# Forty modulation blocks at the start, and gate grids as two rounded products

## The reference, cut to what matters

```
mod = silu(c) @ ada_w[l] + ada_b[l]             # 6 x 1024 values
sh1, sc1, g1, sh2, sc2, g2 = split(mod, 6)
h = rmsnorm(x) * (1 + sc1) + sh1
x = x + g1 * hybrid_mixer(h)                    # four kinds of heads: indexed with a
                                                # T5 bias, rotary latent, forgetting, S5
h = rmsnorm(x) * (1 + sc2) + sh2
x = x + g2 * peer_ffn(h)                        # 128 x 128 experts, 8 heads x top 16
```

## Time and profile before

| what | value |
|---|---|
| median of 3 runs | 2213.9 us (2213.44 to 2215.03) |
| profiled execution, its own time | 2213.12 us |
| span of its instructions | 2211.3 us |
| busy: TensorE, VectorE, ScalarE, GpSimd | 96%, 70%, 56%, 20% |
| transfers | 378.81 MB, mean 171 GB/s |

### The profile page before, as it was taken

How to read it: one execution, slowest core, us unless ns; L and a number is a source line. 1 busy time by engine, 2 the same in 40 slices (tenths; PEclk the granted TensorE clock), 3 DMA queues, 4 the chain that set the end, 5 groups by cost and what they waited for, 6 DMA issues and landing times.

```text
span 2211.3 us, 39875 instructions
## 1 busy us (share of the span) xinstructions
PE 2118.7 (96%) x13716; PEld 1934.7 (87%) x13716; DVE 1543.2 (70%) x3008; ACT 1234.4 (56%) x2348; POOL 440.1 (20%) x184
## 2 busy tenths in 40 slices
PE   5799899999999999999999999999999999999997
PEld 4688789999999998888878978999999998888886
DVE  7688548991778877777768944899177886555554
ACT  8623544554888864444443344455488886545543
POOL 0000046988100000000000005698810000000000
PEclk9899999999999999999999999999999999999999
DMA  7723244555444467777763324455544445666563
GB/s 263 285 81 129 84 139 136 173 169 188 151 137 135 147 201 268 262 261 264 261 213 109 124 68 140 136 171 170 182 153 133 144 142 170 191 194 193 191 193 101
DMA packets 103476, 378.81 MB, mean 171 GB/s; under 512 B 11488, under 2 KB 11872, under 8 KB 102880
## 3 DMA queue, kind: packets, MB, share of 16 engines
q1 hardware_dynamic: 102672, 373.74, 51.2%
q10 hardware_dynamic: 720, 4.00, 0.5%
HBM read 375.46 MB, written 2.23 MB: 171 GB/s over the span
## 4 chain that ended last, share of the span: by engine, by line
PE 74%; issue 9%; POOL 8%; DVE 4%; ACT 2%; DMA 2%; POOLq 0%; ACTq 0%; SPq 0%; DVEq 0%
PE bank L1760 32%; PE bank L1669 8%; PE bank L1670 8%; PE bank L1671 8%; POOL split_lo L478 7%; PE bank L1733 5%; PE bank L1406 4%; DMA ring<-stream 2%; PE bank L1418 1%; PE bank L1657 1%; PE bank L1368 1%; ACT diag L536 1%; PE bank L1431 1%; PE bank L1442 1%; PE bank L1379 1%
## 5 line engine op out<-in xcount | busy, mean ns | idle before, releaser
L1669 PE MATMUL bank<-h_hi,split_hi 128*128 128x256 f32 x2304 | 666.5, 289 | 23.3 <-POOL split_lo L478 11.1
L1671 PE MATMUL bank<-h_hi,split_lo 128*128 128x256 f32 x2304 | 652.1, 283 | 0.0
L1670 PE MATMUL bank<-h_lo,split_hi 128*128 128x256 f32 x2304 | 652.0, 283 | 0.0
L1669 PEld LDWEIGHTS bank<-h_hi,split_hi 128*128 128x128 f32 x2304 | 441.8, 192 | 30.0 <-POOL split_lo L478 16.8
L478 POOL TENSOR_TENSOR split_lo<-ring,split_hi 128x1024 fp32r<-128x1024 f32 x168 | 433.3, 2603 | 172.9 <-ACT split_hi L686 172.7
L1266 DVE TENSOR_TENSOR split_lo<-ring,split_hi 128x1024 fp32r<-128x1024 f32 x248 | 303.8, 1225 | 222.0 <-ACT w_hi L784 222.0
L783 ACT ACTIVATE split_hi<-ring 128x1024 fp32r<-128x1024 f32 x248 | 263.2, 1061 | 343.0 <-PE bank L1760 339.3
L1670 PEld LDWEIGHTS bank<-h_lo,split_hi 128*128 128x128 f32 x2304 | 442.3, 192 | 0.0
L1671 PEld LDWEIGHTS bank<-h_hi,split_lo 128*128 128x128 f32 x2304 | 441.6, 192 | 0.0
L686 ACT ACTIVATE split_hi<-ring 128x1024 fp32r<-128x1024 f32 x296 | 298.7, 1051 | 196.8 <-PE bank L1671 196.7
L1760 PE MATMUL bank<-split_hi,w_hi 128*128 128x512 f32 x1024 | 315.9, 390 | 0.0
(11 more groups left out here) (271 smaller groups left out, 2526.7 us busy)
## 6 DMA issues: line engine op xcount, KB each, us to landing
ring<-stream SPq DMA_DIRECT2D x658, 512.0 KB, 3.5
ada_ring<-stream SPq DMA_DIRECT2D x48, 512.0 KB, 4.3
spill<-tables ACTq DMA_DIRECT2D x1, 1152.0 KB, 4.3
tables<-spill ACTq DMA_DIRECT2D x1, 1152.0 KB, 6.8
xT<-x_in SPq DMA_DIRECT2D x1, 1024.0 KB, 9.5
s5raw<-s5w ACTq DMA_DIRECT2D x2, 512.0 KB, 5.6
y_out<-hT SPq DMA_DIRECT2D x1, 1024.0 KB, 3.9
KM<-mixc SPq DMA_DIRECT2D x1, 576.0 KB, 7.7
```

The source lines that it names most:

```text
L1669: mm(dst, hi, x_hi, start=start, stop=False, skip_group_check=not group)
L1670: mm(dst, hi, x_lo, start=False, stop=False, skip_group_check=not group)
L1671: return mm(dst, lo, x_hi, start=False, stop=stop, skip_group_check=not group)
```

## The change

**Start.** Layer 0's modulation is folded for five chunks only, 40 blocks; the sixth (g2, which is used at the very end of the layer) moves into the value loop of layer 0 ahead of layer 1's six. `pos` and `K` are issued right after `V`, `xT`, `S` and `KM` after the ring. All 31 `ge` have places of their own in `grid`: four are written first, then one after each fold. Chunk sums stand after buckets 10, 15, 20 and 25 and after the last; the squares of x are made by ScalarE after six sets of diagonals and summed after bucket 9, the root stands after twelve sets, and VectorE's norm right behind the folds. The rope arguments go behind the S5 phases, their sine behind `cosT` and ahead of the copy of `aq0`, their products with `mul` ahead of `krA`, and the bias tables (`t5`) behind hT.

**Gate grids.** The gate is split into a rounded high and a low part (VectorE, from PSUM). `hots` are fp32r; `hotA` is scaled by the high part; GpSimd writes four rows a quad scaled by the low part (`hot_lo`, one buffer of four) and waits for the grid before. TensorE makes two rounded products a token that add up in PSUM.

**Value loop.** Turns of 16 rows, seven of them with eight folds each, two accumulators in turn, and each chunk's sums in the middle of the next turn.

```diff
+FIRST_ADA = 5 * KT
+SKIP = ADA - FIRST_ADA
+TURN = 16
@@ sync
             sp.dma_start(V[:, :], vec).then_inc(vec_in, 16)
+            sp.dma_start(posi, pos).then_inc(pos_in, 16)
+            sp.dma_start(K[:, :], consts).then_inc(const_in, 16)
             for s in range(RING):
                 sp.dma_start(ring[:, s, :], stream[s]).then_inc(slot_filled[s], 16)
...
+            sp.dma_start(xT[:, :, :], x_in).then_inc(x_loaded, 16)
+            sp.dma_start(S[:, :, :], small).then_inc(small_in, 16)
             sp.dma_start(KM[:, :], mixc).then_inc(mixc_in, 16)
@@ gpsimd, after the low halves of a layer
+                pool.wait_ge(pick_ready, TT * (l + 1))
+                pool.wait_ge(gates_split, 2 * TT * (l + 1))
+                for q in range(QUADS):
+                    if l or q:
+                        pool.wait_ge(g_ready, QUADS * l + q)
+                    for t in range(4):
+                        at = 4 * q + t
+                        last = gp.tensor_scalar(hot_lo[t], iota, pick[:, 0, at:at + 1], gate_lo[at // P][:, at % P:at % P + 1], ALU.is_equal, ALU.mult)
+                    last.then_inc(lo_hot_ready, 1)
@@ scalar
+            for b in range(6):
+                diagonals(b)
+            act.wait_ge(x_loaded, 16)
+            squares(x_loaded, -1)
...
+            for b in range(6, 12):
+                diagonals(b)
+            root(0, "ss1", D, rstd)
+            for b in range(12, BUCKETS - 1):
+                diagonals(b)
@@ vector
+            for b in range(FIRST_REACHED):
+                reached(b)
+            for n in range(FIRST_ADA):
+                dve.wait_ge(slot_filled[n % RING], 16 * (n // RING + 1))
+                fold(g(ACC0 + n // KT * BLOCK, BLOCK), ring[:, n % RING, :], n % KT, n)
+                if n + FIRST_REACHED < BUCKETS - 1:
+                    reached(n + FIRST_REACHED)
@@ tensor
+            for b in range(BUCKETS - 1):
+                add_bucket(b)
+                if b == 9:
+                    sums_of(0, "ss1", sq, KT, 0)
+                if b in (10, 15, 20, 25):
+                    first_sums((10, 15, 20, 25).index(b))
+            first_sums(FIRST_ADA // KT - 1)
@@ tensor, gate_grids
+                    pe.wait_ge(lo_hot_ready, i * 8 + (q0 + q + 1))
                     for t in range(4):
-                        last = mm(bank[:, 4 + q % 4, t * P:t * P + P], hotB[q % 2][:, t, :], hotA[q % 2][:, t, :], start=True, stop=True)
+                        dst = bank[:, 4 + q % 4, t * P:t * P + P]
+                        mm(dst, hotB[q % 2][:, t, :], hotA[q % 2][:, t, :], start=True, stop=False)
+                        last = mm(dst, hotB[q % 2][:, t, :], hot_lo[t], start=False, stop=True)
```

More of the change, by code:

```diff
@@ L70 @@
 N_BLOCKS = N_MAIN + (DEPTH - 1) * ADA
-ADA_TURNS = (0, 2, 4, 6, 9, 11, 13, 15)
+ADA_TURNS = (0, 2, 4, 6, 8, 10, 12, 13)
+FIRST_ADA = 5 * KT
+SKIP = ADA - FIRST_ADA
+TURN = 16
+LATE_ADA = ADA // KT + 1
+FIRST_REACHED = 4
 EARLY = PQ + KEYS + SPLIT
@@ L568, in _ @@
+                    squares(x_done, l - 1)
+                    root(l, "ss1", D, rstd)
+                act.wait_ge(mods_ready, l + 1)
                 for k in range(KT):
@@ L873, in _, with reached, add_biases @@
-            add_biases(0, 7)
-            dve.wait_ge(rope_sin, 1)
-            for i in range(3):
-                last = v.tensor_scalar(rope[:, i, :], rope[:, i, :], const("mul")[:, i:i + 1], None, ALU.mult)
-            last.then_inc(rope_ready, 1)
-            dve.wait_ge(rope_ready, 1)
-            dve.wait_ge(mixc_in, 16)
+            def reached(b):
+                v.tensor_scalar(ge[:, b, :], dist, K[:, thr + b:thr + b + 1], None, ALU.is_ge).then_inc(ge_ready, 1)
+            def add_biases(l, first, count, biases, sums):
+                link(v.tensor_tensor(mod2[:, l, first:first + count], biases, sums, ALU.add))
@@ L1114, in _ @@
                 maxima(3)
+                if l == 0:
+                    dve.wait_ge(rope_sin, 1)
+                    for i in range(3):
+                        last = v.tensor_scalar(rope[:, i, :], rope[:, i, :], const("mul")[:, i:i + 1], None, ALU.mult)
+                    last.then_inc(rope_ready, 1)
+                    dve.wait_ge(rope_ready, 1)
                 dve.wait_ge(act_taken, taken_count(l, "kr")[1])
@@ L1282, in _, with turn @@
[L1282 to L1288 removed]
+                def turn(i, n, at, chunk):
+                    for j in range(TURN):
+                        low(i, n * TURN, at + j)
+                        if j - 2 in ADA_TURNS:
+                            k = ADA_TURNS.index(j - 2)
+                            dve.wait_ge(ada_filled[k % 2], i * (n * 16 * KT // 2) + 16 * (chunk * KT // 2 + k // 2 + 1))
+                            if k == 0:
+                                dve.wait_ge(ada_columns, i * n + (FIRST_ADA // KT + max(chunk - 1, 0)))
+                            fold(ada_acc[:, chunk % 2, :], ada_ring[:, k % 2, :], k, i * (n * KT) + (FIRST_ADA + chunk * KT + k))
@@ L1289, in _ @@
+                if l + 1 < DEPTH:
+                    turn(0, 1, 0, 0)
+                    with dve.Fori(0, ADA // KT // 2, 1) as i:
+                        turn(i, 2, TURN, 1)
+                        turn(i, 2, 2 * TURN, 2)
+                    for j in range(LATE_ADA * TURN, LATE):
                         low(0, 0, j)
-                    add_biases(l + 1, 0)
+                    dve.wait_ge(ada_columns, FIRST_ADA // KT + LATE_ADA)
+                    add_biases(l, FIRST_ADA, KT, mod2[:, l, FIRST_ADA:ADA], bank[:, 0, 0:KT])
+                    add_biases(l + 1, 0, ADA, small_of(l + 1, "adab"), bank[:, 0, KT:KT + ADA])
```

266 lines of the change are left out of this document (129 added, 137 removed).

## The result

The changed kernel took 2467.1 us (median of 4 runs, 2466.2 to 2468.1), the kernel before, beside it, 2214.5: ratio 1.114, 95% interval 1.112 to 1.116. Slower was forecast, but not by 253 us: 2467 lies far over the range of 2190 to 2330. Medians and ratios here are those of the fast runs; one run of e13, 3457 us at a granted clock of 0.57, is a slow one.

The account below looks back on a forecast made before the run. TensorE, busy 96% of the span, was taken as the bound. 2213.1 - 28.3 + 4.1 + 1.0 + 1.7 + 15.8 + 3.4 + 42.2 = 2253.0, plus 0.8 for the median: 2254 us, range 2190 to 2330.

Parts of the forecast that it names:

- The start: Before the first projection: sums moved between buckets, ScalarE alone paces; first projection at 99.4 instead of 127.7, -28.3 us.
- the wait for `aq0`: After the start: ScalarE waits for VectorE's rope arguments before copying `aq0`, so TensorE waits before `ik`, +4.1 us.
- the inserts: At the start: TensorE's sums between buckets delay ScalarE: 3.3 us after buckets 9 and 10, 0.55 each after 15, 20, 25.
- Gate grids on TensorE: Gate grids: a rounded 128-column product costs 0.113 us like an fp32 pass, so a grid stays 0.90, gain 0.
- B: Gate grids: rounded products cost less, 0.055 to 0.09, and GpSimd's row is cheap; 2167 to 2191 us; chance 0.13.
- C: Gate grids: a rounded 128-column product costs a whole fp32 product, 0.226; +116 instead of 42, 2328 us; chance 0.17.
- The late first grid: First gate grid of each layer: TensorE stands 7.9 us until GpSimd finishes queued low halves and four rows, +15.8 us.
- The row's duration: Gate grids: one scaled row on GpSimd takes 0.39 us, between bounds of 0.10 and 0.84.
- 4 x 0.39 = 1.6 fits, if nothing blocks: Gate grids, steady state: GpSimd's four rows fit in the 2.87 us before TensorE comes back for the next grid.
- The half clock: After each layer's gap before the first gate grid, TensorE runs at clock 0.50 for 3.4 us, +3.4 us in all.
- Who blocks whom: Gate grids: GpSimd's rows hold VectorE up 2.07 us a pair; VectorE becomes the bound at 8.19 against 7.53, +42.2 us.
- D: Gate grids: GpSimd's rows take over 0.5 us, a pair 9.0 or more; 2305 to 2350 us; chance 0.15.

Follow-up runs that it names:

- e13: Changed kernel with VectorE's two late low halves a pair made by one-input products instead of two-input subtractions; 2346.2 us, 1.059.
- e1: Changed kernel with the old gate grids (one fp32 product a token, no GpSimd rows), so new start and value loop alone; 2190.5 us, 0.990.
- e11: e3 without its second product: one rounded product a token, low part of the gates left out; 2135.7 us, 0.965.
- e3: Changed kernel without GpSimd's rows or the wait for them; second rounded product repeats the high row; 2192.9 us, 0.991.
- e4: e1 plus GpSimd rows of several forms into unused space, alone and then beside VectorE rows; the 128-element row took 798 ns alone.
- e9: Changed kernel with two buffers for GpSimd's low rows instead of one, plus two waits a quad for its own rows; 2314.0 us, 1.045.
- e7: Changed kernel with idle TensorE products in the gaps before the gate grids, 9 before odd quads and 3 before even; 2421.6 us, 1.094.
- e14: e9 with VectorE's late low halves made by one-input products instead of two-input subtractions; 2237.2 us, 1.011.
- e10: Changed kernel with GpSimd making only two of the four low rows in each quad after the first; 2279.0 us, 1.030.
- e5: Changed kernel with GpSimd's rows made but awaited by TensorE only after a layer's last grid; GpSimd also awaits its own rows; 2293.0 us, 1.036.

## Why the prediction was wrong

*The start: right.* First projection 99.4 forecast (the terms written there add up to 99.1), 99.2 measured; the wait for `aq0` 4.1 against 3.41, with 1.15 for `du1` that I had not seen; with the chunk in the value loop, -21.5 forecast and -23.7 measured (e1). ScalarE's pace of 2.34 us a bucket and the inserts held.

*Gate grids on TensorE: right.* 0.113 an instruction forecast, 0.112 measured (e11), and +2.4 us in all for the second product and the split (e3). Rivals B and C fall.

*The late first grid: nearly.* 7.9 us a layer forecast, 9.44 measured (`[9.44 <-POOL hot_lo_cd L510]` before the first grid): four rows of 0.79 in place of 0.39.

*The row's duration: the step that failed.* "I take 0.10 + 0.29 = 0.39, the subtraction's own terms." It is 0.79 (e4). I had bounded it at 0.84, with the one-element power of 0.55 as the fixed part, and then took the set's 0.10, a row with no input and no scalar. The operation has two operations and two per-partition scalars, so the power was nearer in kind. From this followed the second mistake, "4 x 0.39 = 1.6 fits, if nothing blocks": 3.27 for four rows and the 1.33 until GpSimd may begin are 4.6, and a quad of TensorE has 3.77. Nothing in the text asked what happens where it doesn't fit, though the kernel has one buffer: then TensorE and GpSimd take turns. One buffer costs at least 153 us (e9 against after), the rate with the late first rows at most 121 (e9 against e3), as e9's own pauses are in it. The half clock, 45 of the loss (e7), was forecast as 3.4, for the first gap alone. Added up from the rows, as an estimate: e7's pair is 3.16 over the 7.53 of before, 202 in 64 pairs; with 45 for the clock and 19 for the first grids that is 266 of the 274. Of the 202, 0.83 a quad, 106, are the undisturbed circle, and the rest the rows that VectorE lengthens.

*Who blocks whom: mostly the wrong way round.* The 42 us were to be VectorE held up by GpSimd. VectorE's work grew by 7 us a layer; GpSimd was held up, by VectorE's subtractions with two SBUF inputs, 77 us of e9's 121 (e14 against e9). The rows of before that I read as a blocking of all sorts lie beside a two-input subtraction of GpSimd; one-input rows of 128 elements on both engines run nearly free (e4), but one-input products of 1024 on VectorE do not (a row of 1.52 in e14). The Trainium skill, in *SBUF — State Buffer*, section "Who interferes with whom", draws this line itself, which I passed over: it has a VectorE instruction with two SBUF inputs contend with a GpSimd one that reads SBUF, and one with at most one such input not, outside VectorE's faster two-port modes. On two inputs the runs agree: two rows took 3.46 for 1.70 in e10. On one input the line decides less, as the same section of the Trainium skill lists `tensor_scalar` among the instructions that can enter those modes, and no view here names the mode: 0.34 stayed 0.34 in e4, and yet a one-input row took 2.43 beside GpSimd's subtraction. By e4 most of the 2.07 us a pair of my sum should not have stood there, and GpSimd's rows should have carried the 2.47 of the late low halves.

*The rivals.* D, rows over 0.5, had the right cause and the wrong price: it used the formula of a bound on VectorE and stopped at 2350. The same formula with 0.79 gives 10.99 us a pair and 2213.1 - 21.5 + 15.8 + 3.4 + 221 = 2432. That is close by accident, since e5 shows that VectorE bounds nothing. But the range was thereby not what my own bounds made it: 0.84 stood in the text, and 2330 as the upper end answers to about 0.56.

## What to carry to other kernels

Before work goes to an engine that is idle, write down the circle: who frees the buffer, how long the helper takes by its dearest near row, and who starts after it. If that circle with one buffer is longer than the main engine's step, the difference is paid at every step, whatever the busy shares say, and the clock's fall comes on top. When an experiment takes the circle apart, look for what its own edit adds to the helper's work (here 0.27 us of pauses a quad). Choose the helper's form of instruction by measurement (here two rows in one two-input product of 0.61 against two rows of 0.79 each), and let the range reach as far as the dearest bound in the text.

## What the runs showed of the hardware

- GpSimd's row of 128 elements, two operations with two per-partition scalars: 0.80 us; one operation 0.60; fixed numbers 0.64; a two-input product 0.46, and 0.61 for 256 elements (e4). A one-element instruction of that form costs 0.38, where GpSimd's set of one element took 0.10.
- VectorE's one-input rows of 128 elements and GpSimd's run beside each other at nearly full speed (0.34 and 0.86, e4); beside one-input products of 1024 elements a row of GpSimd took 1.52 (e14), and beside subtractions of 1024 with two SBUF inputs up to 3.2 us (e9).
- A rounded product of 128 columns takes 0.112 us (e11), so two of them cost what one fp32 product does (e3 against e1): splitting an operand gains TensorE nothing here, leaving its low part out does.
- Gaps of 0.6 to 2.7 us in every quad, 5.7 us long in the mean, went with a granted clock of 0.88, that is half clock for a quarter of the time, and idle products in them brought it back to 0.99 (e7).
